# Six small matmul groups of the attention, each moved by one block of the input projection

## What is computed

```python
def _token_mix(h, pos, lambda_init, w_in, w_out, g_qk, w_lambda, g_sub, kv_past, s0):
    rq, rk, rv, rg, dq, dk, dv = jnp.split(h @ w_in, split_points, axis=-1)
    rq = _rotary(rq, pos, ret_freq, True)
    rk = _rotary(rk, pos, ret_freq, True) * (RET_DK ** -0.5)
    o_r, s_new = _retention(rq, rk, rv, s0)
    o_r = _rms_norm(o_r) * jax.nn.silu(rg)
    dq, dk = _rotary(_rms_norm(dq, g_qk[0]), ...), _rotary(_rms_norm(dk, g_qk[1]), ...)
    # k_all, v_all: the cache (512 keys, sample only), then dk, dv
    o_d = _diff_attention(dq, k_all, v_all, lam, pos, k_pos)   # (softmax(q1 k1) - lam * softmax(q2 k2)) v
    o_d = _rms_norm(o_d, g_sub) * (1.0 - lambda_init)
    mix = jnp.concatenate([o_r, o_d], axis=-1) @ w_out
```

## Time and profile before

| what | value |
|---|---|
| median of 3 runs | 1364.43 us (1364.16 to 1366.07) |
| the profiled execution: time, span | 1366.7 us, 1364.9 us |
| busy share PE, DVE, ACT, POOL | 98%, 71%, 42%, 30% |
| chain that ended last | PE 94%, DVE 2%, DMA 2%, SPq 1%, POOL 1% |
| granted TensorE clock, mean | 0.996 |
| the projection in layer 0, in layer 1 | from about 300 to 418 us, from about 963 to 1084 us |

### The profile page before, as it was taken

One profiled execution on the slowest core, in us unless ns is written; L12 is line 12 of the kernel. 1 busy time (PEld: TensorE's weight loads), 2 busy tenths in 40 slices (PEclk: granted clock), 3 DMA queues, 4 the chain that ended last, 5 costly groups with the idle time before them and its releaser, 6 DMA issues.

```text
span 1364.9 us, 23813 instructions
## 1 busy us (share of the span) xinstructions
PE 1339.9 (98%) x9479; PEld 1224.7 (90%) x9479; DVE 964.2 (71%) x1502; ACT 571.3 (42%) x976; POOL 405.2 (30%) x285
## 2 busy tenths in 40 slices
PE   6999999999999999999999999999899999999998
PEld 4999999986778999999999999999576799999998
DVE  3588866557676978777657878654677688988743
ACT  4333434234555534334434334432454544344421
POOL 1233333412102433334423333433021133333421
PEclk8999999999999999999999999999999999999999
DMA  9999677716323789756568886674344246666651
GB/s 334 316 292 293 178 248 212 228 57 217 132 93 101 242 281 290 227 141 186 146 200 278 260 253 183 167 212 154 124 140 150 93 132 177 180 185 170 170 161 48
DMA packets 327789, 261.13 MB, mean 191 GB/s; under 512 B 8816, under 2 KB 288960, under 8 KB 327552
## 3 DMA queue, kind: packets, MB, share of 16 engines
q1 hardware_dynamic: 326592, 256.47, 61.8%
q0 software_dynamic: 1088, 3.15, 0.6%
HBM read 255.12 MB, written 4.46 MB: 190 GB/s over the span
## 4 chain that ended last, share of the span: by engine, by line
PE 94%; DVE 2%; DMA 2%; SPq 1%; POOL 1%; DVEq 0%; issue 0%; ACT 0%; ACTq 0%
PE ps L657 24%; PE ps L659 23%; PE ps L658 23%; PE ps L683 3%; PE ps L889 3%; PE ps L852 3%; PE ps L894 3%; PE ps L890 3%; DMA arena<-in_cache_k 1%; PE ps L819 1%; PE ps L915 1%; PE ps L773 1%; PE ps L772 1%; PE ps L777 1%; PE ps L654 1%; SPq L514 1%
## 5 line engine op out<-in xcount | busy, mean ns | idle before, releaser
L1466 DVE TENSOR_TENSOR w_lo<-raw,w_hi 128x1024 fp32r<-128x1024 f32 (+3 forms) x304 | 477.7, 1612 | 74.5 <-ACT w_hi L1164 73.5
L657 PE MATMUL ps<-h_hi,w_hi 128*128 128x322 f32 x1344 | 420.0, 313 | 0.0
L659 PE MATMUL ps<-h_hi,w_lo 128*128 128x322 f32 x1344 | 417.1, 310 | 0.0
L658 PE MATMUL ps<-h_lo,w_hi 128*128 128x322 f32 x1344 | 416.4, 310 | 0.0
L1164 ACT ACTIVATE w_hi<-raw 128x1024 fp32r<-128x1024 f32 (+1 forms) x304 | 324.5, 1115 | 200.3 <-PE ps L659 182.4
L1977 POOL TENSOR_TENSOR w_lo<-raw,w_hi 128x512 fp32r<-128x512 f32 (+1 forms) x112 | 209.9, 1874 | 612.6 <-ACT w_hi L1164 612.6
L657 PEld LDWEIGHTS ps<-h_hi,w_hi 128*128 128x128 f32 x1344 | 253.3, 188 | 10.5 <-issue 10.5
L658 PEld LDWEIGHTS ps<-h_lo,w_hi 128*128 128x128 f32 x1344 | 254.3, 189 | 0.0
L659 PEld LDWEIGHTS ps<-h_hi,w_lo 128*128 128x128 f32 x1344 | 252.6, 188 | 0.0
L1228 ACT ACTIVATE t_buf<-t_buf,shift_w 128x256 f32<-128x256 f32 (+1 forms) x176 | 65.9, 422 | 392.9 <-DVE t_buf L1556 392.9
L657 PE MATMUL ps<-g_hi,w_hi 128*128 128x320 f32 x704 | 217.7, 309 | 0.0
(11 more groups left out here) (191 smaller groups left out, 1481.2 us busy)
## 6 DMA issues: line engine op xcount, KB each, us to landing
raw<-in_w_ff_up SPq DMA_DIRECT2D x176, 512.0 KB, 5.3
ada_raw<-in_w_ada SPq DMA_DIRECT2D x102, 512.0 KB, 6.6
raw<-in_w_ff_down SPq DMA_DIRECT2D x64, 704.0 KB, 6.6
raw<-in_w_in SPq DMA_DIRECT2D x48, 512.0 KB, 4.0
half_raw<-in_w_ada SPq DMA_DIRECT2D x64, 256.0 KB, 5.2
raw<-in_w_out SPq DMA_DIRECT2D x16, 512.0 KB, 4.0
first_raw<-in_w_ada SPq DMA_DIRECT2D x10, 512.0 KB, 9.8
arena<-in_cache_k SPq DMA_DIRECT2D x2, 1024.0 KB, 7.2
```

The costliest lines, as they stand in the source:

```text
L657: pe.matmul(out, hi, mhi, start=start, stop=False)
L658: pe.matmul(out, hi, mlo, start=False, stop=False)
L659: return pe.matmul(out, lo, mhi, start=False, stop=stop)
L1466: dve.tensor_tensor(w_lo[s % 2][:, cols], raw[s % 2][:, cols], w_hi[s % 2][:, cols], ALU.subtract)\
```

## The change

Six entries of three tables grow by one, so that six groups of PE's list move behind one block, in each of the two layers:

```diff
-TURN_AT = [10, 12, 14, 16, 17, 18, 19, 21, 24, 27, 38, 39, 42]
+TURN_AT = [10, 12, 14, 16, 17, 18, 19, 21, 24, 27, 38, 40, 42]
 SCORES_AT = [22, 26, 30, 34, 38]
-PROBS_AT = [27, 31, 35, 40, 44]
+PROBS_AT = [27, 32, 36, 40, 44]
 TURN_OWN_AT = [36, 40]
-WEIGH_AT = [29, 33, 37, 42, 45]
+WEIGH_AT = [30, 34, 38, 42, 45]
```

## The result

The changed kernel takes 1374.39 us (median of 6 runs, 1371.23 to 1376.17); the kernel before, in 6 runs (the three of the prediction and three more), 1365.94 (1364.16 to 1366.75). The ratio is 1.0062, with a 95% interval from 1.0051 to 1.0073: slower by 8.45 us, or 7.0 to 10.0 by the interval. The profiled execution takes 1374.19 us with a span of 1372.4.

A forecast was written before the change was run, and what follows sets the result against it. PE, busy 1339.9 of 1364.9 us, was taken to bound the kernel. Per layer 1.42 + 0.94 + 1.15 - 0.2 = 3.3 us slower, 6.6 in two layers: 1364.43 + 6.6 = 1371.0 us, range 1368.0 to 1374.0.

The forecast's parts named there:

- the third pause: PE at q = 42: turn 12 waits for copy_probs(3), held up on ACT behind turn 11's copy; 1.15 us per layer.
- The base: Whole kernel: the median of 1364.43 us before the change, to which the forecast added 6.6 us.
- Gain: six handovers fewer: PE, blocks behind the six moved groups: fewer slow starts, 0.2 us per layer saved, between 0 and 0.5.
- five of the six groups ... I give them 0.02 each: PE, moved groups beside 64-wide matmuls of another shape: each saves 0.02 us; weigh(2) alone saves all 0.08.
- all is paid back: PE, the six moved groups: lower end of the handover gain, 0 us saved per layer.
- The pauses: PE waits for ACT copies at q = 32, q = 40 and q = 42: 1.42, 0.94 and 1.15 us per layer.
- the 0.06 us from the end of ACT's copy to PE: ACT to PE at each new wait: PE sees a copy's end 0.06 us later.
- the second: PE at q = 40: turn_probs(3) waits for ACT's copy of turn 11, same bank; 0.94 us per layer.
- The hidden copies: Rival, whole stage: copies are hidden, only handovers show, 0 to 0.5 us per layer won, 1364.4 to 1363.4; chance 0.05.
- the place at q = 40 alone: Rival: block q = 32 does not wait, only turn 11's place costs, 3.8 us in all, 1368.2; chance 0.04.
- a further wait: Rival: PE pauses again behind DVE's wait for copy_out(7) or at q = 43, about 1 us per layer, 1373.0; chance 0.07.
- The clock: Rival: TensorE's clock falls to 1.2 GHz in the six pauses, costing 17 us, 1388; chance 0.04.

The follow-up runs named there:

- experiment 1: Changed kernel with turn_probs(1) moved back from q = 32 to q = 31: 1369.84 us, ratio to the kernel before 1.0038.
- experiment 2: Changed kernel with turn 11 moved back from q = 40 to q = 39: 1367.81 us, ratio to the kernel before 1.0020.
- experiment 4: Changed kernel with copy_out(7) put ahead of copy_probs(1) on ACT, PE's order unchanged: 1371.24 us, ratio to the kernel before 1.0040.
- experiment 5: Changed kernel with copy_out(9) put ahead of turn 11's copy on ACT: block q = 27 to output mix 59.17 us in layer 0, for 60.15.
- experiment 3: Changed kernel with both turn_probs(1) and turn 11 moved back: 1365.51 us, ratio to the kernel before 1.0001.
- experiment 7: experiment 3 with only the semaphore waits of weigh(0) and weigh(1) issued ahead of the scores: block q = 27 to output mix 56.14 us, for 56.37.
- experiment 10: experiment 7 with weigh(1) at q = 34 put behind the own scores: block q = 27 to output mix 55.85 us, for 56.14.
- experiment 8: Changed kernel with turn 12's wait for copy_probs(3) put last among its waits: block q = 27 to output mix 60.00 us, for 60.15.
- experiment 9: experiment 8 without the count behind the wait for copy_probs(3): block q = 27 to output mix 59.92 us, for 60.00.
- experiment 11: Changed kernel with turn 11 and turn_probs(2) back, weigh(0) and weigh(1) ahead of scores, copy_out(7) ahead of copy_probs(1): 1364.32 us, ratio to kernel before 0.9997.
- experiment 6: experiment 3 with weigh(0) and weigh(1) put ahead of the scores at q = 30 and 34: block q = 27 to output mix 55.79 us, for 56.37.

## Why the prediction was right in its mechanism and wrong in its size

**What held.** That the change is slower, that it is PE that pauses, at which three places, for which copies of ACT, and that the third pause lies at q = 42 behind a list of ACT. Experiments 1, 2, 4 and 5 moved each of these by itself and gave the stretch that the mechanism asks for to within 0.15 us. The wait of L889 was there under another name than forecast, "issue". Also right: the first intervals of the blocks q = 29, 31, 33, 35, 37 and 39 fell from between 0.31 and 0.34 us to between 0.22 and 0.24; PE has no further wait at q = 34, 36 or 43; and the second layer repeats the first. The pauses were paid in full, as said, as far as the times can tell: 8.43 us in the two stretches, 7.0 to 10.0 by the interval of the times.

**What failed.** The time is 3.4 us above the forecast of 1371.0, and 0.4 outside the range. That has three parts. Neither the first alone (1365.94 + 6.6 = 1372.5) nor the other two alone (1364.43 + 8.43 = 1372.9) would have left it.

*The base.* The forecast added 6.6 us to a median of three runs, 1364.43. In the six runs beside the changed kernel it was 1365.94. These 1.5 us are no statement about the change, and later medians of the kernel before lie between the two (1365.59 of 20 runs, 1365.16 of 15); a range for a time that is added to a median of three needs the spread of that median, and mine had none.

*Gain: six handovers fewer.* Forecast -0.2 us per layer, between 0 and -0.5; measured +0.36 in layer 0. The failed step is "five of the six groups ... I give them 0.02 each", and the end at 0, "all is paid back". The row behind it is of transposes behind the sample matmuls, and for the groups that got that place it was about right: +0.03 for `turn_probs(2)`, and -0.06 and -0.07 for `turn_probs(1)` and turn 11 without their pauses (1.40 - 1.46, 0.96 - 1.03). `weigh(2)` gave -0.18, twice what I gave it. But `weigh(0)` and `weigh(1)` went behind and between score groups, of which no row existed, and there the price is a loss: +0.22, and +0.34 for `weigh(1)` (the piece takes 5.84 us in experiment 3, where the block q = 32 does not wait, for 5.50 before; the other 0.05 of the table's 0.39 is that block's second tile). Experiments 7 and 10 show the two causes apart: the time of three semaphore waits that no long matmul covers (0.20 of the 0.22 went when they were issued earlier), and a 128-row group between two 64-row groups (0.33 of the 0.34 went when it was put behind both). I had closed the range at 0 where no row excluded a loss.

*The pauses.* Forecast 1.42, 0.94 and 1.15, measured 1.46, 1.03 and 1.33: 0.3 us per layer too little. The failed step is the 0.06 us from the end of ACT's copy to PE. It was read off a matmul with nothing left to do behind its wait, and was used for waits that have a count behind them (`turn_probs(3)`: copy's end 402.95, matmul 403.09, 0.14) or a count, a second wait and its count (turn 12: 0.29). Experiments 8 and 9 took these away in two steps: 0.29, 0.15, 0.05. With 0.14 and 0.29 in place of 0.06 the second and the third pause of the prediction's sum come out at 1.02 and 1.30.

Together 0.56 + 0.31 in layer 0 and a little more in layer 1: 8.43 us against 6.6. With the 1.5 of the base that is the 3.4.

**The rivals.** The hidden copies, the place at q = 40 alone and a further wait are out by the table of waits above and experiments 1 to 3. The clock did not fall in the new pauses. The windows over the stretch in both layers, after (start:end, length, busy us and instructions of PE, PEld, DVE, ACT, POOL, granted clock, DMA share, GB/s):

```profile
362.00:424.00 62.00, 58.40 (x385) 41.45 (x384) 36.91 (x89) 29.12 (x73) 3.33 (x5) 1.00 0.29 100
1030.00:1092.00 62.00, 58.34 (x386) 41.49 (x386) 36.87 (x89) 29.43 (x74) 2.74 (x3) 1.00 0.29 97
```

The granted clock is 1.00, the level of 2.4 GHz, through pauses of up to 1.22 us of idle time right at transposes. The place that bears most on this rival stood in the trace before, and the prediction priced the rival without it: the wait of 2.1 us for the cache's load, in layer 1, ahead of the moved groups. Timeline of PE and windows, before:

```profile
987.76 0.66 PE L819 MATMUL ps<-tab,arena 128*128 128x128 f32 x4 [2.07 <-DMA arena<-in_cache_k]
...
988.00:990.00 2.00, 2.00 (x10) 1.67 (x9) 1.85 (x5) 0.60 (x1) 0.00 (x0) 0.79 0.09 33
990.00:992.00 2.00, 2.00 (x6) 1.55 (x5) 1.93 (x3) 0.00 (x0) 0.00 (x0) 0.50 0.00 0
992.00:994.00 2.00, 2.00 (x14) 1.01 (x15) 1.78 (x5) 1.14 (x2) 0.00 (x0) 0.85 0.00 0
```

Behind this pause, four transposes and the start of a block, the granted clock was at 0.50, the level of 1.2 GHz, and back at 1.00 some 3 us later. So the clock does fall behind single pauses of this kernel, and the rival was a real one; the three pauses of the change did not bring it about in any kept trace. The length of the pause alone does not decide: at the same place the clock fell behind 2.07, 1.88 and 2.15 us (the kernel before, experiments 4 and 7) and stayed at 1.00 behind 2.40 and 1.84 (experiments 8 and 11). What else decides was not tested. The Trainium skill, "TensorE: Matmul & The Clock Gate", "Why this matters for your kernels", warns of idle gaps longer than those of the change, so these neither bear it out nor speak against it, and the prediction stretched it when it let the rule stand for this rival.

## What to carry to other kernels

Before a group is moved past work on an engine that is full, follow what it feeds on the other engines to the end of their lists: a copy that stands in an in-order list ahead of something the full engine needs turns a harmless place into a pause, and it can show two blocks later. Where a handover has no row of its own kind (the shape before, the shape after, the number of waits between), leave the sign open. For effects below the spread of the time, measure a stretch of the timeline that holds all that moves: it repeated to 0.11 us or better from layer to layer here, where the times of one kernel spread by 3 us and more.

## What the runs showed of the hardware

**Semaphore instructions on PE have a price that matmuls hide.** Each wait or count behind the wait that ends last cost 0.07 to 0.10 us (0.29, 0.15 and 0.05 us with three, one and none behind it), and three waits with their counts ahead of `weigh(0)` showed as 0.22 us behind the short own scores (experiment 7). Behind a block of 512-column matmuls they showed as nothing: the last two matmuls of the block take 0.47 us up to `weigh(0)` before the change (366.75 to 367.22), and 0.47 up to the next block after it (368.26 to 368.73).

**A change between 64-row and 128-row matmuls costs about 0.1 to 0.3 us.** The eight 128-row matmuls of L968 take 0.80 us between blocks of their own shape, 0.91 behind the own scores and ahead of a block (369.78 to 370.69 in experiment 7), 0.98 up to the scores and 1.09 up to the own scores of 64 rows. The Trainium skill, "TensorEngine Tiling (Array Packing)", "Key Properties", says that a change of the tiling mode drains TensorE; the rows agree that it costs, and the size is theirs. The 0.98 is the same with two waits ahead of the scores (q = 30) and with one (q = 34, 381.74 to 382.72 in experiment 6). How much of the 1.09 is the wait ahead of the own scores was not taken apart, nor which of the rows, the columns and the width of the matmuls makes the cost, since they change together here.

**A fall of the clock behind one pause cost 1.6 us.** From the end of the stretch in layer 0 to its start in layer 1 it takes 606.12 to 606.15 us less the wait for the cache's load, in the ten kept traces where the granted clock stays at 1.00 there, and 607.68 to 607.70 in the three where it falls to 0.50 behind that wait.
